# Two diagonals of a pair of expert slots: one broadcast product on VectorE, or two scaled copies on ScalarE

## What is computed

```python
a = jnp.einsum("td,tkd->tk", xb, expert_u[eid]).astype(jnp.float32)
w = (jax.nn.gelu(a, approximate=False) * gate).astype(xb.dtype)
return jnp.einsum("tk,tkd->td", w, expert_v[eid])
```

## Time and profile before

| | us |
|---|---|
| median of 3 runs | 4599.48 (4595.16 to 4602.47) |
| span of the profiled execution | 4597.2 |
| TensorE, matmuls busy | 3084.2 |
| VectorE busy | 3112.0 |
| ScalarE busy | 906.1 |
| GpSimd busy | 1510.9 |

### The profile page before, as it was taken

How to read it: one execution, slowest core, us unless ns; L and a number is a source line. 1 busy time by engine, 2 the same in 40 slices (tenths; PEclk the granted TensorE clock), 3 DMA queues, 4 the chain that set the end, 5 groups by cost and what they waited for, 6 DMA issues and landing times.

```text
span 4597.2 us, 49199 instructions
## 1 busy us (share of the span) xinstructions
PE 3084.2 (67%) x16384; PEld 1197.3 (26%) x16384; DVE 3112.0 (68%) x8352; ACT 906.1 (20%) x2464; POOL 1510.9 (33%) x1378
## 2 busy tenths in 40 slices
PE   8889996757885455554665786778885555545554
PEld 4445444312231111111221222555331111111111
DVE  2352337878778778777878764634687877877886
ACT  2442212111111111111111111541121111111211
POOL 0000113444443444444434332010344444444443
PEclk9989999878997777777887898997996777787767
DMA  4342228999999999999999996121999999999998
GB/s 157 123 165 92 78 78 323 415 414 400 418 418 396 414 417 408 418 415 403 387 419 395 414 400 232 35 97 69 359 408 400 408 419 415 405 419 411 397 418 348
DMA packets 307838, 1517.96 MB, mean 330 GB/s; under 512 B 26272, under 2 KB 94368, under 8 KB 143744
## 3 DMA queue, kind: packets, MB, share of 16 engines
q0 software_dynamic: 185888, 1347.13, 71.3%
q1 hardware_dynamic: 87616, 133.07, 8.4%
q10 hardware_dynamic: 34080, 34.62, 2.2%
HBM read 1498.51 MB, written 16.20 MB: 329 GB/s over the span
## 4 chain that ended last, share of the span: by engine, by line
DVE 40%; PE 28%; DMA 19%; issue 7%; ACT 4%; POOL 1%; DVEq 1%; ACTq 0%; POOLq 0%; SPq 0%
DMA X<-in_uv_dram,X 17%; DVE X L2041 16%; PE ps L1121 7%; PE ps L580 6%; DVE X L2052 2%; ACT X L1572 2%; PE ps L1038 1%; DVE X L1942 1%; DVE X L1940 1%; DVE X L1943 1%; DVE X L2048 1%; PE ps L1104 1%; PE ps L915 1%; PE ps L803 1%; POOL X L2175 1%
## 5 line engine op out<-in xcount | busy, mean ns | idle before, releaser
L1121 PE MATMUL ps<-X 64*64 64x512 f32 x2560 | 1628.7, 769 | 1269.7 <-DVE X L2052 1256.1
L2175 POOL DMA_INDIRECT X<-in_uv_dram,X x1280 | 1429.8, 1117 | 2168.8 <-PE ps L1124 1698.7
L2041 DVE CUSTOM_DVE_ANT_0 X<-yT,X 128x1024 f32<-128x1024 f32 x1280 | 1531.1, 1223 | 319.3 <-DMA X<-in_uv_dram,X 269.9
L1122 PE MATMUL ps<-X 64*64 64x512 f32 x2560 | 1628.8, 770 | 0.0
L1124 PE MATMUL ps<-X 64*64 64x512 f32 x2560 | 1628.8, 770 | 0.0
L1123 PE MATMUL ps<-X 64*64 64x512 f32 x2560 | 1628.8, 770 | 0.0
L1121 PEld LDWEIGHTS ps<-X 64*64 64x64 f32 x2560 | 358.3, 162 | 2442.9 <-DVE X L2052 1746.0
L1572 ACT ACTIVATE X<-X 128x1 f32<-128x1 f32 x1280 | 256.5, 202 | 2279.4 <-DVE X L2041 2214.7
L1124 PEld LDWEIGHTS ps<-X 64*64 64x64 f32 x2560 | 358.5, 162 | 0.0
L1122 PEld LDWEIGHTS ps<-X 64*64 64x64 f32 x2560 | 358.4, 162 | 0.0
L1123 PEld LDWEIGHTS ps<-X 64*64 64x64 f32 x2560 | 358.4, 162 | 0.0
(11 more groups left out here) (293 smaller groups left out, 3569.8 us busy)
## 6 DMA issues: line engine op xcount, KB each, us to landing
wring<-in_ada_w_dram SPq DMA_DIRECT2D x48, 1024.0 KB
wring<-in_w_in_dram SPq DMA_DIRECT2D x36, 1024.0 KB
wring<-in_peer_wq_dram SPq DMA_DIRECT2D x24, 1024.0 KB
X<-in_uv_dram,X POOLq DMA_INDIRECT x1280
wring<-in_w_out_dram SPq DMA_DIRECT2D x8, 1024.0 KB
X<-scores ACTq DMA_DIRECT2D x64, 128.0 KB
X<-mods ACTq DMA_DIRECT2D x15, 512.0 KB, 8.5
ahead<-X ACTq DMA_DIRECT2D x18, 256.0 KB
```

The source lines that it names most:

```text
L1121: pe.matmul(ps[0:HD, h, :], dg(slice(0, HD), s), v0[0:HD], **ends)
L1122: pe.matmul(ps[HD:P, 2 + h, :], dg(slice(HD, P), s), v0[HD:P], **ends)
L2041: v.tensor_tensor_reduce(uvr[:, slot, 0:D], h2[:, t, :], uvr[:, slot, 0:D], 1.0, 0.0, ALU.mult, ALU.add, adot[:, s_:s_ + 1]).then_inc(S("d ...
L2175: g.indirect_dma_start(uvr[:, slot, :], None, a["uv"], bass.IndirectOffsetOnAxis(ap=istages[i % 2][:, s:s + 1], axis=0)).then_inc(S(f"uv{s ...
```

## The change

The product on VectorE is taken out, with its two waits. ScalarE builds the diagonals instead: after the gelus of a pair it waits for the weights ("wt") and for the `dgs` slots ("em"), and writes each diagonal with one Copy of `ident2` whose scale operand is the column of the weights, one number per partition. The second copy raises "dg". The other work that ScalarE has in the pair stands behind these copies.

```diff
@@ expert_gelus, on ScalarE
                             nc.scalar.activation(agel[:, s:s + 1], adot[:, s:s + 1], ACT.Gelu).then_inc(S("gel"), 1)
+                        act.wait_ge(S("wt"), B("wt", L) + (SLOTS // BATCH) * i + q + 1)
+                        if q * BATCH >= DGRING:
+                            act.wait_ge(S("em"), B("em", L) + (SLOTS // BATCH) * i + (q * BATCH - DGRING) // 2 + 1)
+                        for s in range(q * BATCH, (q + 1) * BATCH):
+                            m = nc.scalar.activation(dgs[:, s % DGRING, :], ident2, ACT.Copy, scale=adot[:, s:s + 1])
+                        m.then_inc(S("dg"), 1)
                         if i == 0 and q in (1, 2, 4, 5):
                             store_scores(first, 0, (1, 2, 4, 5).index(q))
@@ tile_body, on VectorE
                         v.tensor_tensor(adot[:, both], agel[:, both], gstage[:, both], ALU.mult).then_inc(S("wt"), 1)
-                        if s_ >= DGRING:
-                            v.wait_ge(S("em"), B("em", L) + NQ * i + (s_ - DGRING) // 2 + 1)
-                        v.wait_ge(S("wt"), B("wt", L) + NQ * i + q + 1)
-                        v.tensor_tensor(dgs[:, s_ % DGRING:s_ % DGRING + BATCH, :], ident2.unsqueeze(1).to_broadcast([P, BATCH, HD]),
-                                        adot[:, both].unsqueeze(2).to_broadcast([P, BATCH, HD]), ALU.mult).then_inc(S("dg"), 1)
                         if i and q == 1:
                             accumulate(i - 1)
```

## The result

The changed kernel takes 4574.7 us (median of 4 runs, 4571.12 to 4576.31), the kernel before 4599.42. The ratio is 0.9943, with a 95% interval from 0.9931 to 0.9955. It is faster by 24.7 us, where the forecast was 9. The span of the profiled run is 4569.3 us, 27.9 under that of before; this run is the shortest of the four.

The account below looks back on a forecast made before the run. Gathers of expert rows were taken to pace both stages, with VectorE's backlog setting the gaps. Seams 6.0, other gaps 3.5 and small windows 1.2, less 1.1 and 0.4, gave 9 us: about 4590.5 us, range 4580 to 4606.

Parts of the forecast that it names:

- S: VectorE time freed per pair, start to start, by removing the product: 0.35 us (0.32 to 0.39), 224 us over 640 pairs.
- D: Added latency per pair from VectorE's weights to TensorE's start, through ScalarE's copies: +0.22 us (+0.12 to +0.44).
- A table load per copy: Rival: ScalarE copies need another table than gelu, two loads per pair, at least 30 us slower; chance under 0.03.
- The ceiling: Most the change can win: DMA share missing up to 1.00 over both expert stages, 36.7 us in some 27 gaps.
- the sum: Gains at seven seams 6.0, seven other gaps 3.5, small windows 1.2, less 1.1 and 0.4: 9.2 us, rounded to 9.
- the larger gain: Rival: VectorE's backlog is four or five pairs, half of the 36.7 us is won, 18 us, 4581 us; chance 0.15.
- about 27: Expected sign: the sum of the DMA shortfall over the stages falls to about 27 us in place of 36.7.
- k: Pairs of VectorE backlog before a gap; buffers come free k x S - D earlier, about 0.5 us for k = 2.
- recovery of a seam: VectorE's catching up behind a tile seam's first gap: 0.35 us more, making 0.85 us at each of seven seams.
- "Nothing": Rival: TensorE and GpSimd end the gaps, so the gain is 0 to 3 us, 4598 us; chance 0.13.
- both slower cases: Rivals: hand-over decides, 14 us slower, 4613 us; or table loads per copy, at least 30 us slower; together 0.12.
- The store of scores: On ScalarE, a store VectorE waits for stands behind the copies, 0.85 us later; price with D 1.1 us.

Follow-up runs that it names:

- e3: Changed kernel with two extra, unread copies on ScalarE ahead of each pair's real ones; 4582.65 us, ratio 0.9963 to the kernel before.
- e1: Changed kernel with VectorE also making the old product, with its two waits, into an unread tile; 4604.93 us, ratio 1.0013 to the kernel before.
- e2: Changed kernel with VectorE still waiting for the weights to be written, without the product; 4579.33 us, ratio 0.9957 to the kernel before.
- e4: Changed kernel with the product of gelu and gate also moved to ScalarE; 4566.22 us, ratio 0.9926 to the kernel before.
- e5: Changed kernel, but ScalarE makes diagonals only for the 12 pairs around a tile's seam, VectorE the other 52; 4589.01 us, ratio 0.9975 to the kernel before.
- e6: Changed kernel, but ScalarE makes diagonals only for the 52 pairs away from the seam, VectorE the 12 around it; 4581.01 us, ratio 0.9958 to the kernel before.
- e9: Changed kernel, but ScalarE makes diagonals only for 32 pairs a tile, those with selection behind them and the next; 4581.83 us, ratio 0.9961 to the kernel before.
- e10: Changed kernel, but ScalarE makes diagonals only for the 32 pairs with q % 8 of 1 to 4; 4591.95 us, ratio 0.9983 to the kernel before.
- e7: Changed kernel with a layer's first four stores of scores issued before the pair's two copies; 4576.61 us, ratio 0.9951 to the kernel before.
- e8: Changed kernel with gelu, gate product and diagonal done slot by slot on ScalarE; 4564.53 us, ratio 0.9928 to the kernel before.

## Why the prediction was wrong

- **The bound was right.** Gathers pace both stages, and only time that reaches a gap counts: about 30 us of gain for 253 us freed on VectorE.
- **S was nearly right.** 0.35 us (0.32 to 0.39) were predicted, and 0.40 (0.48 to 0.08) measured in 600 pairs, 0.33 in 40. The small product and its successor lie 0.08 us apart, against 0.09 from L1957's row. The prediction had both distances, 0.48 and 0.41, but didn't see that the difference was the wait on "em", and said that this wait "costs nothing before". It cost 0.07 us a pair.
- **The copies and D were right.** 345 ns predicted, 340 measured; two copies 0.59 us, against 0.57. From L2048's successor L2054 to TensorE 0.83 us, as predicted, so D = +0.22. A table load per copy: fell, the counts are the same.
- **The ceiling was wrong.** "That is the most that the change can win", 36.7 us, rested on the DMA share. By bytes the gaps held 70.9 us. The forecast of 9 lay far under either, so this step didn't make the sum too small; it made the price of the larger gain too low and, afterwards, a fall to 26.0 by share look like the forecast come true ("about 27").
- **k was wrong, and is the term that was mis-sized.** k is the number of pairs of backlog whose freed time adds up before a gap. The sum took k = 2 (0.50 us a gap, and 0.35 more in the recovery of a seam: 0.85). The measured prices give an average of it. A microsecond of hand-over costs 17 us (e3), a microsecond freed in every pair gains 30.2 / 0.395 = 76 us (0.395 is 253 / 640). Their ratio is 4.5 pairs. Put into the prediction's own formula, 17 x (4.5 x 0.395 - 0.22) = 26 us; that this comes near the gain is no test, as 17 and 4.5 were taken from the same runs. Nor is 76 a constant: by e1, e2 and e4 it is some 90 us for the product and its wait on "em", 40 for the other wait and 30 for what e4 frees.
- **Why k was misread.** The prediction took the wait of 0.56 us at 1426.04 as proof that VectorE had caught up there, so that what was freed earlier was lost. Set side by side, the weights' products of the two kernels around that seam say otherwise. Before:

```profile
1421.59 0.16 DVE L2048 TENSOR_TENSOR X<-X 128x2 f32<-128x2 f32 x1 [0.27 <-ACT X L1572]
...
1432.85 0.16 DVE L2048 TENSOR_TENSOR X<-X 128x2 f32<-128x2 f32 x1 [0.27 <-ACT X L1572]
```

Changed:

```profile
1420.44 0.16 DVE L2054 TENSOR_TENSOR X<-X 128x2 f32<-128x2 f32 x1 [0.27 <-ACT X L1572]
...
1423.92 1.23 DVE L2047 CUSTOM_DVE_ANT_0 X<-yT,X 128x1024 f32<-128x1024 f32 x1
...
1425.42 0.16 DVE L2054 TENSOR_TENSOR X<-X 128x2 f32<-128x2 f32 x1 [0.27 <-ACT X L1572]
...
1430.39 0.16 DVE L2054 TENSOR_TENSOR X<-X 128x2 f32<-128x2 f32 x1 [0.27 <-ACT X L1572]
...
1442.38 0.16 DVE L2054 TENSOR_TENSOR X<-X 128x2 f32<-128x2 f32 x1
...
1445.77 0.16 DVE L2054 TENSOR_TENSOR X<-X 128x2 f32<-128x2 f32 x1 [0.27 <-ACT X L1572]
```

The changed kernel leads by 1.15 us at the first, 2.12 at the second (1427.54 in the earlier trace rows), 2.46 at the third and 2.99 at 1445.37. The step of 0.97 us is the 0.40 freed (here 0.48 less 0.08) and the wait of 0.56 together: that gather comes in time now (1423.92 follows without a wait). It is the 254th in order in both traces. Before, GpSimd issued it in a row of issues that began when TensorE's products released the first of them:

```profile
1404.44 1.75 POOL L2175 DMA_INDIRECT X<-in_uv_dram,X  x1 [8.12 <-PE ps L1124]
...
1412.06 0.94 POOL L2175 DMA_INDIRECT X<-in_uv_dram,X  x1 [0.30 <-issue]
```

Changed:

```profile
1408.49 0.94 POOL L2176 DMA_INDIRECT X<-in_uv_dram,X  x1 [1.83 <-PE ps L1124]
```

It went out 3.57 us sooner. So a wait for a gather doesn't end a backlog if the gather itself was issued late, because earlier pairs gave their buffers back late.

What the whole seam gains can be read at gathers for which VectorE waits in both kernels. Before:

```profile
1420.08 1.23 DVE L2041 CUSTOM_DVE_ANT_0 X<-yT,X 128x1024 f32<-128x1024 f32 x1 [1.25 <-DMA X<-in_uv_dram,X]
...
1506.72 1.23 DVE L2041 CUSTOM_DVE_ANT_0 X<-yT,X 128x1024 f32<-128x1024 f32 x1 [1.26 <-DMA X<-in_uv_dram,X]
```

Changed:

```profile
1418.94 1.23 DVE L2047 CUSTOM_DVE_ANT_0 X<-yT,X 128x1024 f32<-128x1024 f32 x1 [1.25 <-DMA X<-in_uv_dram,X]
...
1502.51 1.23 DVE L2047 CUSTOM_DVE_ANT_0 X<-yT,X 128x1024 f32<-128x1024 f32 x1 [1.27 <-DMA X<-in_uv_dram,X]
```

The lead grows from 1.14 to 4.21 us: 3.1 us at a seam that the sum had at 0.85 (at one gather such a lead swings by about 1 us). And in the kernel before, VectorE waits for no gather from 1426.04 to 1495.22, 13 pairs on end. The prediction looked at the pairs ahead of the gap and let the backlog end soon behind it; but VectorE stays behind through the recovery too, and with it pairs without selection count. That this explains all of k is argued from one seam; e5, e6, e9 and e10 show only that the gain isn't bound to seams and is larger behind the selection.
- **The rivals.** The larger gain was the nearest: a backlog of four or five pairs, half the gaps filled. It had 0.15. Its price, half of the shortfall by share, was 18 us; by bytes the change filled 27.9 of 70.9 us, which is 39% and not half. "Nothing" and both slower cases fell. e1 is what the slower case looks like when VectorE wins nothing: 4.4 us slower, not 14, in line with a hand-over paid at some 17 places and a D of 0.22.
- **The store of scores** waited 1.3 us longer, 1.1 predicted, and e7 shows that the total doesn't feel it.
- **The Trainium skill's page** ScalarE: Activation LUTs (What ACT_TABLE_LOAD costs) has a formula that makes an estimate of 332 ns for such a copy; the trace has 340. The page also puts a switch of tables at about 2.66 us, of which the load itself is 1283 ns and the rest a drain. In e8 a load starts 0.02 us behind the end of the copy before it, and a gelu 1.29 us after the start of the load (1439.34 to 1440.63). So the trace agrees on the load and shows no drain at this place, and by it the switch costs 1.3 us.

## What to carry to other kernels

Where a ring of buffers is fed by gathers and one engine falls behind now and then, price an edit by two numbers: what it frees on that engine in every step, and what it adds to the hand-over that gives the buffer back. The first adds up over all the steps of a backlog, and those behind the gap, in which the engine is still catching up, are among them; the second was paid about once a gap here. Count the gaps of the transfers in bytes against the best windows, not by the share of busy time, and don't take a short wait for a transfer as the end of a backlog until you have seen when that transfer was issued.

## What had not been expected of the hardware

- A window in which the DMA engines are busy for 0.96 of the time can move 324 GB/s, where full ones have a median of 420. The stages, at a share of 1.00 on average, still lacked 2% by bytes (70.9 of 3250 us).
- A wait of VectorE on its own last instruction costs more than it seems: 0.12 us a pair in e2, and some 5 us of the total.
- A second wait ahead of the same instruction, on a semaphore that another engine raises, cost VectorE 0.07 us a pair in the kernel before (0.27 against 0.20 us from L2048 to L2052).
